# A two-block transformer kernel: diagonal Gram blocks, their inverses on TensorE, and gates scaled on VectorE

## What is computed

```python
# mixer: two attention outputs, each projected up and gated, then projected out
y = jax.nn.sigmoid(gate_a) * (o_nsa @ w_up_nsa) + jax.nn.sigmoid(gate_b) * (o_fox @ w_up_fox)
return y @ w_out

# RWKV-7 state recurrence, per head
S = S * w_t[:, :, None, :] + sa[..., None] * b_t[:, :, None, :] + v_t[..., None] * k_t[:, :, None, :]
y = jnp.einsum('bhvk,bhk->bhv', S, r_t)      # with sa = S a_t
```

## Time and profile before

| | us |
|---|---|
| median of 3 runs (1684.64 to 1693.65) | 1691.85 |
| profiled execution, device time | 1692.82 |
| its span | 1691.5 |
| TensorE busy | 1517.3 (90%) |
| VectorE busy | 985.0 (58%) |
| ScalarE busy | 702.0 (41%) |
| GpSimd busy | 20.2 (1%) |
| mean granted clock of TensorE | 0.926 of full |

### The profile page before, as it was taken

The page is one execution under the profiler, slowest core; times in us unless marked ns, Lnnn a source line. Parts: engine busy times, 40 slices in busy tenths (PEclk is TensorE's granted clock), DMA queues, the critical chain, the costliest instruction groups (busy, mean ns, idle before and its releaser), DMA issues. The chain is left out here.

```text
span 1691.5 us, 27780 instructions
## 1 busy us (share of the span) xinstructions
PE 1517.3 (90%) x12196; PEld 1446.6 (86%) x12196; DVE 985.0 (58%) x1291; ACT 702.0 (41%) x1058; POOL 20.2 (1%) x19
## 2 busy tenths in 40 slices
PE   8999999999699899999899641996999998799999
PEld 8999998787699899999798341886899997689999
DVE  5665653457564456555565579425656665766565
ACT  5444542345454344444353400223544453454443
POOL 0000000000200000000000010000000000000000
PEclk9999998899999999999799655797999998999999
DMA  6555462420345144555242000002455441044552
GB/s 251 201 191 182 180 220 76 174 101 1 125 154 195 51 156 182 189 183 190 77 175 100 25 1 0 26 1 103 147 199 178 175 172 50 24 152 180 195 195 80
DMA packets 33025, 222.26 MB, mean 131 GB/s; under 512 B 3887, under 2 KB 5167, under 8 KB 6536
## 3 DMA queue, kind: packets, MB, share of 16 engines
q1 hardware_dynamic: 31848, 219.42, 36.3%
q10 hardware_dynamic: 1056, 1.07, 0.2%
HBM read 219.40 MB, written 1.06 MB: 130 GB/s over the span
## 5 line engine op out<-in xcount | busy, mean ns | idle before, releaser
L304 DVE TENSOR_TENSOR tile_lo<-ring,tile_hi 128x1024 fp32r<-128x1024 f32 x396 | 478.4, 1225 | 410.1 <-ACT tile_hi L294 409.3
L294 ACT ACTIVATE tile_hi<-ring 128x1024 fp32r<-128x1024 f32 x396 | 409.7, 1054 | 358.2 <-PE ps L346 311.5
L344 PE MATMUL ps<-hT_hi,tile_hi 128*128 128x256 f32 x1600 | 454.8, 284 | 9.7 <-DVE hidden_lo L753 7.6
L345 PE MATMUL ps<-hT_lo,tile_hi 128*128 128x256 f32 x1600 | 452.1, 283 | 0.0
L346 PE MATMUL ps<-hT_hi,tile_lo 128*128 128x256 f32 x1600 | 452.0, 283 | 0.0
L344 PEld LDWEIGHTS ps<-hT_hi,tile_hi 128*128 128x128 f32 x1600 | 305.4, 191 | 13.4 <-DVE hidden_lo L753 8.0
L346 PEld LDWEIGHTS ps<-hT_hi,tile_lo 128*128 128x128 f32 x1600 | 305.1, 191 | 0.0
L345 PEld LDWEIGHTS ps<-hT_lo,tile_hi 128*128 128x128 f32 x1600 | 305.1, 191 | 0.0
L346 PE MATMUL ps<-hidden_hi,tile_lo 128*128 128x256 f32 x864 | 243.3, 282 | 0.0
L344 PE MATMUL ps<-hidden_hi,tile_hi 128*128 128x256 f32 x864 | 243.1, 281 | 0.0
L345 PE MATMUL ps<-hidden_lo,tile_hi 128*128 128x256 f32 x864 | 243.1, 281 | 0.0
(11 more groups left out here) (436 smaller groups left out, 2337.9 us busy)
## 6 DMA issues: line engine op xcount, KB each, us to landing
ring<-stream SPq DMA_DIRECT2D x204, 1024.0 KB, 4.8
x_sb<-x SPq DMA_DIRECT2D x4, 256.0 KB, 4.1
bias<-f_dram ACTq DMA_DIRECT2D x1, 1024.0 KB, 8.5
squares<-mem SPq DMA_DIRECT2D x1, 1024.0 KB, 4.8
cum<-rows SPq DMA_DIRECT2D x1, 1024.0 KB
out<-x_sb SPq DMA_DIRECT2D x4, 256.0 KB, 2.0
small_sb<-small SPq DMA_DIRECT2D x1, 485.5 KB, 8.7
const_sb<-const SPq DMA_DIRECT2D x1, 385.0 KB, 9.0
```

The lines of the kernel that those rows point to most:

```text
L294: act.activation(e.w_hi[:, n % SPLIT, :], e.ring[:, tile % RING, span(n % 2, HALF)], ACT.Copy).then_inc(e.tile_hi.handle, 1)
L304: dve.tensor_tensor(e.w_lo[:, n % SPLIT, :], e.ring[:, CUT[n // 2] % RING, span(n % 2, HALF)], e.w_hi[:, n % SPLIT, :].bitcast(F32), ALU.s ...
L344: pe.matmul(out, left[0], right[0], start=start, stop=False)
L345: pe.matmul(out, left[0], right[1], start=False, stop=False)
```

## The change

- `rwkv_inverses`: TensorE first makes the 32 by 32 diagonal blocks of each Gram matrix by products of their own, 64 rows by 32 columns, in two banks. VectorE masks them in two forms (`gd`, `gu`), one transpose of 128 partitions turns all, and `solve_blocks` stops at inverses of the blocks of 16. Two transposes of 128 partitions place them (`t16`, `a16`). TensorE makes the inverses of 32 from them (identity plus `gu` times `t16`, then times `a16`), in products of 32 by 32. The full Grams are made meanwhile and copied by ScalarE without a mask, columns 32 and up. The transposes of b and k move ahead, and 40 filler products follow them. Copies are split over ScalarE and VectorE. `unit_of` orders the units by head parity first.
- `up_stage`: the scaling of the gates moves from GpSimd to VectorE, the block becomes `Open`, and the next stage's TensorE waits for each piece of y (`y_split`).
- `attention_stage`: at step `ahead` ScalarE and VectorE split the tiles of the stage that follows as far as the buffers allow (for the mixer step 5, for the other two step 1).
- `values`: products of the two halves of 64 partitions alternate.
- a constant `block_keep` of 64 columns, and one operation in `rwkv_prepare` that makes the mask of it.

```diff
@@ out_stage, TensorE
             for i in range(4):
+                if ready:
+                    pe.wait_ge(*ready.since(i + 1))
                 row_to_T(e, pe, g0 + i, src, 2 * i, i == 0, i == 3)
@@ attention_stage
+    ahead = min(len(fillers) + 1, n - 1)
...
                     act.activation(dst, e.ps[:, 7, :], ACT.Copy).then_inc(*filled.one())
+                if step == ahead:
+                    heads_after(e, act, 2 * follows)
...
                 if step < len(fillers):
                     rests_before(e, dve, fillers[step][0] + 1)
+                if step == ahead:
+                    rests_after(e, dve, 2 * follows)
@@ fox_unit, values (nsa_unit and swa_unit likewise)
-        for par in range(2):
-            for cc in range(2):
-                head = 2 * (2 * j + cc) + par
-                for kb in range(t + 1):
-                    mm = pe.matmul(out[par * HD:(par + 1) * HD, cc * P:(cc + 1) * P],
...
+        for cc in range(2):
+            for kb in range(t + 1):
+                for par in range(2):
+                    head = 2 * (2 * j + cc) + par
+                    lasts[par] = pe.matmul(out[par * HD:(par + 1) * HD, cc * P:(cc + 1) * P],
...
@@ up_stage
-    with nc.Block() as block, ExitStack() as stack:
+    with Open(nc) as block:
...
-        @block.gpsimd
-        def _(pool):
-            for n in range(4):
-                for half in range(2):
-                    at = 8 * half + 2 * n
-                    pool.tensor_tensor(m.ab[:, at:at + 2, :], m.ab[:, at:at + 2, :], scale_pairs(e),
-                                       ALU.mult).then_inc(*gate_scaled.one())
...
-                                  flat(m.y[0][:, 2 * n:2 * n + 2, :]).bitcast(F32), ALU.subtract)
-
+                                  flat(m.y[0][:, 2 * n:2 * n + 2, :]).bitcast(F32), ALU.subtract).then_inc(*y_split.one())
+
+            for n in range(4):
+                for half in range(2):
+                    at = 8 * half + 2 * n
+                    dve.tensor_tensor(m.ab[:, at:at + 2, :], m.ab[:, at:at + 2, :], scale_pairs(e),
+                                      ALU.mult).then_inc(*gate_scaled.one())
@@ rwkv_inverses, TensorE
+            for i in range(UNITS // 2):
+                for q in range(QS):
+                    for par in range(2):
+                        b, ar = operands(16 * par + i, rows(q), rows(q))
+                        mm = pe.matmul(e.ps[rows(q), par, span(i, BLK)], b, ar, start=True, stop=True)
+            mm.then_inc(*diag_done.one())
+            for i in range(4):
+                if i == 2:
+                    pe.wait_ge(*diag_read.at(2))
+                for k in range(4):
+                    for par in range(2):
+                        b, ar = operands(16 * par + 4 * i + k, slice(0, P), slice(0, P))
+                        mm = pe.matmul(e.ps[:, (4 * par + i + 2) % 8, span(k, P)], b, ar, start=True, stop=True)
+                mm.then_inc(*gram_done.one())
             for n in range(4):
+                pe.wait_ge(*gram_copied.at(2 * n + 1))
...
+            pe.wait_ge(*gram_copied.at(8))
+            keep_busy(e, pe, 40, 7)
             pe.wait_ge(*copied.at(4))
+            pe.wait_ge(*t16_placed.at(1))
+            for g in range(2):
+                for s in range(16 * g, 16 * g + 16):
+                    for q in range(QS):
+                        out = e.ps[rows(q), 2 * q + g, span(s % 16, BLK)]
+                        pe.matmul(out, ident[rows(q), rows(q)], ident[rows(q), rows(q)], start=True, stop=False)
+                        mm = pe.matmul(out, gu[rows(q), s, :], t16[rows(q), s, :], start=False, stop=True)
+                mm.then_inc(*step_done.one())
+            pe.wait_ge(*a16_placed.at(1))
+            for g in range(2):
+                pe.wait_ge(*step_copied_a.at(2 * g + 1))
+                pe.wait_ge(*step_copied_b.at(2 * g + 1))
+                for s in range(16 * g, 16 * g + 16):
+                    for q in (0, 2):
+                        mm = pe.matmul(e.ps[rows(q), 2 * q + g, span(s % 16, BLK)], a16[rows(q), s, :], step[rows(q), s, :],
+                                       start=True, stop=True)
+                mm.then_inc(*t32_done.one())
+            for g in range(2):
...
+                for s in range(16 * g, 16 * g + 16):
+                    at = span(s % 16, BLK)
+                    pe.matmul(e.ps[rows(1), g, at], step[rows(1), s, :], a16[rows(1), s, :], start=True, stop=True)
+                    pe.matmul(e.ps[rows(3), 4 + g, at], step[rows(3), s, :], a16[rows(3), s, :], start=True, stop=True)
+                    pe.matmul(e.ps[rows(1), 6 + g, at], v.gram[rows(0), s, rows(1)], v.turned[rows(0), s, 0:BLK],
+                              start=True, stop=True)
+                    mm = pe.matmul(e.ps[rows(3), 2 + g, at], v.gram[rows(2), s, rows(3)], v.turned[rows(2), s, 0:BLK],
+                                   start=True, stop=True)
+                mm.then_inc(*narrow_done.one())
...
@@ rwkv_inverses, VectorE
+            dve.wait_ge(*diag_done.at(1))
+            for n, dst in enumerate((gd, gu)):
+                for g in range(2):
+                    x = dve.tensor_tensor(dst[:, units(g), :].bitcast(I32),
+                                          e.ps[:, g, :].rearrange("p (s n) -> p s n", s=16).bitcast(I32), kept(n), ALU.bitwise_and)
+                x.then_inc(*diag_read.one())
+            dve.wait_ge(*diag_read.at(1))
+            link.done(dve.transpose(v.n.rearrange("p j i -> p i j"), gd.rearrange("p s i -> p i s")))
             solve_blocks(link, v).then_inc(*solved.one())
             dve.wait_ge(*solved.at(1))
+            dve.transpose(t16.rearrange("p s j -> p j s"), v.inv).then_inc(*t16_placed.one())
+            dve.transpose(a16[:, :, :].rearrange("p s i -> p i s"),
+                          v.inv.rearrange("p j i -> p i j")).then_inc(*a16_placed.one())
@@ solve_blocks
-    while half < BLK:
+    while half < BLK // 2:
```

More of the change, by code:

```diff
@@ L2209, in rwkv_inverses @@
     wide_copied = [e.sig("wide_copied_act"), e.sig("wide_copied_dve")]
-    strict = w.mask[:, 0, :].unsqueeze(1).to_broadcast([P, 4, P])
     rows = lambda q, n=1: slice(q * BLK, (q + n) * BLK)
-    with nc.Block() as block:
+    units = lambda g: span(g, UNITS // 2)
+    kept = lambda n: w.block[:, n, :].unsqueeze(1).to_broadcast([P, UNITS // 2, BLK])
+    ident = const(e, "ident")
+    blocks = lambda bank, q: e.ps[rows(q), bank, :].rearrange("p (s n) -> p s n", s=UNITS // 2)
+    place = lambda s: (s % (TT * PAIRS) // PAIRS, s // (TT * PAIRS), s % PAIRS)
@@ new lines, in _ @@
+            for g in range(2):
+                pe.wait_ge(*cross_copied_a.at(2 * g + 2))
+                pe.wait_ge(*cross_copied_b.at(2 * g + 2))
+                for s in range(16 * g, 16 * g + 16):
+                    at = span(s % 16, BLK)
+                    pe.matmul(e.ps[rows(2), g, at], step[rows(2), s, :], a16[rows(2), s, :], start=True, stop=True)
+                    mm = pe.matmul(e.ps[rows(0), 2 + g, at], step[rows(0), s, :], a16[rows(0), s, :], start=True, stop=True)
+                mm.then_inc(*late_done.one())
@@ L2337, in _ @@
+                copy(v.full[rows(2), units(g), rows(3)], blocks(2 + g, 2)).then_inc(*cross_copied_b.one())
+            for g in range(2):
+                dve.wait_ge(*late_done.at(g + 1))
+                copy(v.full[rows(0), units(g), rows(0)], blocks(2 + g, 0)).then_inc(*late_copied_b.one())
             for g in (1, 3):
-                wide_copy(dve, dve.tensor_copy, g)
+                wide_copy(dve, copy, g)
             for g in (1, 3):
-                last_copy(dve, dve.tensor_copy, g)
+                last_copy(dve, copy, g)
```

215 lines of the change are left out of this document (102 added, 113 removed).

## The result

The changed kernel takes 1678.06 us in the median of 6 runs (1673.34 to 1681.65), beside 1693.12 of the kernel before in its 6 runs. The ratio is 0.9914, with a 95% interval of 0.9893 to 0.9935: about 15 us faster, between 11 and 18. The forecast was 1668 us, 24 us faster; the range of 1650 to 1684 holds the result. The profiled execution is the slowest of the six (1681.65 us, span 1680.3), 3.6 us above the median.

What follows compares the result with a forecast made beforehand. Span mostly dense products; the main target was the unhidden TensorE-VectorE chain of the inverses. Terms: 17.6 + 10.5 + 3.3 - 5.0 - 2.4 - 0.1 = 23.9 us, giving 1668 us; range of 8 in 10: 1650 to 1684.

Steps and rivals of the forecast that it cites:

- a case of late products: Inverses: fillers at half clock hold the chain 8 us, or products cost 50 ns; 1676 to 1677 us, chance 0.16.
- Inverses, in front of the small products: Inverses up to the first placed blocks: diagonals 4.1 us, one transpose 2.1, last solver level gone; gain 27.8 us.
- Inverses, the small products: Inverses after the placed blocks: 768 products for 160; 10 of 27.8 us given back, stage gain 17.6 us.
- At 32 ns a product: Inverses: price of overlapping small products, 107 ns for each on the same tile at half clock.
- narrow: Small-product group of the inverses, priced at 2 x 2.05 = 4.1 us.
- cross: Small-product group of the inverses, two of its four in one tile, priced at 2 x 3.5 = 7.0 us.
- late: Small-product group of the inverses, priced at 3.7 us.
- the rival with full clock: Inverses: clock stays at 2.4 GHz through the small products, 12 us less; 1656 us, chance 0.12.
- Slower than before: Inverses: small products do not overlap, each costs 107 ns in turn; 51 us more, 1719 us, chance 0.06.
- Up and output stages: Gates moved to VectorE 3.1 us earlier, output tiles started per piece of y without barrier; together 10.5 us gain.
- Attention: Interleaved values against the early split: mixer 3.3 us gain, memory attention 5 us loss, window attention 2.4 loss.
- The hold: Attention stages: early split makes VectorE wait before the reciprocal for ScalarE's head; held 4.3 us.

Runs made afterwards that it cites:

- The folded kernel: Changed kernel with the step's 128 identity products folded into an operand that GpSimd forms while VectorE solves; ratio 0.9902 to the kernel before.

## Why the prediction was right, and where it was not

**The time.** Right in sign, in the range, and 10 us too good. The range held because it reached to a case of late products (1676 to 1677), whose size was about right and whose causes were not those at work: the fillers did not come late, and the products lost their time in the pauses. That part was luck.

**Inverses, in front of the small products.** Right: masks, one transpose at 2.1 us, the solver's first part unchanged, the last level gone. The diagonals took 4.8 us and not 4.1, and they are the first place where the pause shows: 256 records, two bursts with 1.8 us between. The fillers end with the transposes, as said.

**Inverses, the small products.** This is the step that failed: "At 32 ns a product", for the step and the narrow products above all. The 32 ns were read from 64 products that came after TensorE had stood still for 38 us and made 16 transposes. They show what TensorE does with instructions that it already has. A neighbouring row had the other number, in its last column: 2.50 us at 7 GB/s is about 17 KB, one packet for 128 records. A stage with 1280 records in a row takes ten of them, and 3.6 us for 128 records is 56 ns a product. By the starts of the groups, with the sum's figure behind each:

| group | measured us | sum | ns a product in the sum |
|---|---|---|---|
| step | 12.4 | 8.2 | 32 |
| 32-blocks | 3.9 | 3.7 | 58 |
| narrow | 7.1 | 4.1 | 32 |
| cross | 8.7 | 7.0 | 55 |
| late | 4.0 | 3.7 | 58 |

Where the sum took 32 ns it is short by 7.2 of the 9.4 us. The other groups came out nearly right by accident: their 55 to 58 ns stood for products that exclude each other on a tile, and what is measured is 49 to 68 ns by group, 56 in the mean. It was a mis-sized term, in a mechanism (small products give back part of what VectorE wins) that was right: they gave back 19 us, not 10. (The step starts 26.5 us earlier in its stage than the first small product did before, and the stage is 7.1 shorter.)

**The clock.** It was 0.50 through cross, late and wide, as said. But half of the 12 us that the rival with full clock promised were not to be had: with the clock at 0.50 from the first step product the stretch is as long as with 1.00 at its start, so there, it is to be expected, TensorE would only have waited longer for instructions. The other 6, in the wide products, where no pause of over 0.5 us stands, were not tried.

**Slower than before.** The rival's threshold was 63 ns a product. The products came to 56, and the runs point to another reason than tiles that exclude each other. That case was nearer than its 0.06 suggests.

**Up and output stages.** Right in each piece: 11.4 us for 10.5, 3.4 of it the gates (3.1) and 8.0 the barrier (7.4).

**Attention.** The hold was 4.3 us where it was read, 3.09 of wait and 1.23 of work, in the mixer and in memory attention (4.0 in the window attention). Memory attention lost 6.9 for the 5 of the sum: the window from 567.1 to 577.3 shows the clock down, as the working had feared, where it was 1.00 before (566 to 577). VectorE's hold there, and the window:

```profile
568.04 1.23 DVE L304 TENSOR_TENSOR tile_lo<-ring,tile_hi 128x1024 fp32r<-128x1024 f32 x1 [3.09 <-ACT tile_hi L294]
...
567.10:577.30 10.20, 5.51 (x25) 5.14 (x26) 3.68 (x11) 2.95 (x3) 0.00 (x0) 0.50 0.00 0
```

In the mixer's second part, the one that the edits reach, the interleaved products won 8.2 us alone (7.6 in the sum), the split lost 6.5 alone (4.3), and together they gained 3.2 (3.3). Beside the interleaved products the split costs 4.8 us (59.9 against 55.1), near the 4.3 of the hold. So the sum was right for the two together. The 1.9 us of the whole stage are these 3.2 less 1.3 in the first part, where the clock was 0.86 instead of 0.92. The folded kernel, whose edit doesn't touch this stage, shows 78.0 us instead of 82.3; of these 4.3 us, 2.8 lie in that first part, which ran at a clock of 1.00. The profiled execution being the slowest of its six explains why the profiled executions differ by 11 us and the medians by 15.

**What stays open.** That the time follows the packets is shown by their number, in three sizes, and by their landing before each burst. Why the next packet comes no sooner, no run tried. Why the clock is 1.00, 0.92 or 0.86 in the mixer's first part with the same code is open too.

## What to carry to other kernels

Count instructions, not only engine time: before moving work from one engine to many tiny products, divide their number by what one packet of instructions holds and multiply by the time per packet that the trace shows (here 128 records and 3.6 us). A rate read from a short burst after an idle stretch is no rate for a long one. And an operation put in front of another in an engine's order "to be ready early" is only worth it if someone waits for it later; here the stage behind lasted 52.28 us with it and without.

## What the runs showed of the hardware

- TensorE's instructions come in packets of 16,384 bytes, 128 matmuls with their weight loads. A long run of small products took 3.5 to 3.7 us for each 128 records, about 28 ns a record, whatever the clock (3.54 at half clock, 3.61 with the first part at full); packets started 3.4 to 4.4 us apart, and a burst 1.2 to 1.6 us after one had landed.
- Once they are there, matmul records of 32 by 32 tiles follow each other at 9.6 ns at a clock of 1.00 and at 13.5 ns at 0.50, both below what the prediction took (16).
- A block transpose of 1024 elements per partition takes 2.0 to 2.1 us on 128 partitions as on 32.
- A VectorE operation with two inputs, started while GpSimd ran one of its own on 128x1024 elements, ended with it: 0.18 us became 1.88. A transpose, with one input, did not last longer (2.15 and 2.13).
- The same stretch of the mixer's attention, reached by no edit, took 19.6 us at a granted clock of 1.00, 21.2 at 0.92 and 22.4 at 0.86. Its clock is to be looked at before the lengths of two executions are compared.
